# Two fused transformer blocks on one Trainium2 core: up projections as a run of 512-column and a run of 256-column matmuls per weight chunk

## What is computed

```python
# first block
h = rms_norm(x, pre_ffn_norm)
u = causal_dwconv(h @ w_up, conv_w, conv_b)        # w_up: 2048 x 11264
gate, up = jnp.split(u, 2, axis=-1)
y = (jax.nn.gelu(gate, approximate=True) * up) @ w_down
x = x + rms_norm(y, post_ffn_norm)
# second block
up = dwconv3(h @ w_in, w_conv)                     # w_in: 2048 x 11264
gate, val = jnp.split(up, 2, axis=-1)
y = (jax.nn.silu(gate) * val) @ w_out
```

## Time and profile before

| | |
|---|---|
| Median of three runs | 2491.46 us (2490.28 to 2492.52) |
| The profiled execution's own time | 2501.78 us |
| Its span | 2500.0 us, mean granted TensorE clock 0.998 |
| TensorE matmul busy | 2482.6 us, 14809 instructions |
| TensorE weight loads busy | 2108.4 us |
| VectorE, ScalarE, GpSimd busy | 1860.7, 1359.7, 164.2 us |
| Read from HBM | 462.59 MB, 188 GB/s over the span |

### The profile page before, as it was taken

How to read it: one execution, slowest core, us unless ns; L and a number is a source line. 1 busy time by engine, 2 the same in 40 slices (tenths; PEclk the granted TensorE clock), 3 DMA queues, 4 the chain that set the end, 5 groups by cost and what they waited for, 6 DMA issues and landing times.

```text
span 2500.0 us, 37782 instructions
## 1 busy us (share of the span) xinstructions
PE 2482.6 (99%) x14809; PEld 2108.4 (84%) x14809; DVE 1860.7 (74%) x2240; ACT 1359.7 (54%) x1810; POOL 164.2 (7%) x82
## 2 busy tenths in 40 slices
PE   9999999999999999999999999999999999999998
PEld 8888888888888888888888888888888888888886
DVE  6676775787777879888485868775667777678987
ACT  6565664645555555555545455554555555555554
POOL 1000000020111200000000000000012121120000
PEclk9999999999999999999999999999999999999999
DMA  8875445666666666656655555555666666666664
GB/s 239 257 207 151 119 141 185 213 184 186 180 190 186 183 203 223 213 191 207 191 172 168 170 160 170 161 160 180 204 190 190 188 188 189 193 188 224 218 214 158
DMA packets 259266, 470.69 MB, mean 188 GB/s; under 512 B 14520, under 2 KB 56817, under 8 KB 257985
## 3 DMA queue, kind: packets, MB, share of 16 engines
q1 hardware_dynamic: 256897, 457.64, 59.2%
q0 software_dynamic: 2144, 11.30, 1.5%
q10 hardware_dynamic: 96, 0.02, 0.0%
HBM read 462.59 MB, written 6.32 MB: 188 GB/s over the span
## 4 chain that ended last, share of the span: by engine, by line
PE 96%; DVE 1%; DMA 1%; ACT 1%; issue 0%; DVEq 0%; ACTq 0%
PE acc L336 13%; PE tp L336 13%; PE acc L316 7%; PE acc L318 7%; PE acc L317 7%; PE tp L338 7%; PE acc L338 7%; PE acc L1389 4%; PE acc L619 3%; PE acc L618 3%; PE acc L620 3%; PE acc L1391 2%; PE tp L632 1%; PE tp L633 1%; PE tp L634 1%; PE acc L1639 1%
## 5 line engine op out<-in xcount | busy, mean ns | idle before, releaser
L303 DVE TENSOR_TENSOR whl<-raw,whl 128x1024 fp32r<-128x1024 f32 x679 | 877.3, 1301 | 460.1 <-ACT whl L298 458.6
L298 ACT ACTIVATE whl<-raw 128x1024 fp32r<-128x1024 f32 x679 | 717.5, 1060 | 783.9 <-PE acc L338 227.0
L336 PE MATMUL acc<-ahl,whl 128*128 128x512 f32 x1408 | 494.4, 395 | 0.6 <-DVE ahl L421 0.6
L336 PE MATMUL tp<-ahl,whl 128*128 128x512 f32 x1408 | 494.2, 395 | 0.0
L338 PE MATMUL tp<-ahl,whl 128*128 128x256 f32 x1408 | 394.8, 280 | 0.0
L338 PE MATMUL acc<-ahl,whl 128*128 128x256 f32 x1408 | 394.7, 280 | 0.0
L336 PEld LDWEIGHTS acc<-ahl,whl 128*128 128x128 f32 x1408 | 264.0, 187 | 62.8 <-issue 1.0
L336 PEld LDWEIGHTS tp<-ahl,whl 128*128 128x128 f32 x1408 | 263.9, 187 | 61.9
L316 PE MATMUL acc<-whl,ahl 128*128 128x512 f32 x752 | 298.9, 398 | 1.9 <-DVE ahl L2274 1.5
L318 PE MATMUL acc<-whl,ahl 128*128 128x512 f32 x752 | 293.4, 390 | 0.0
L317 PE MATMUL acc<-whl,ahl 128*128 128x512 f32 x752 | 292.8, 389 | 0.0
(11 more groups left out here) (342 smaller groups left out, 3569.8 us busy)
## 6 DMA issues: line engine op xcount, KB each, us to landing
raw<-in_w_up_dram SPq DMA_DIRECT2D x176, 512.0 KB, 4.3
raw<-in_ffn_w_in_dram SPq DMA_DIRECT2D x176, 512.0 KB, 4.3
raw<-in_hgrn_w_in_dram SPq DMA_DIRECT2D x160, 512.0 KB, 3.7
raw<-in_w_in_dram SPq DMA_DIRECT2D x87, 512.0 KB, 3.7
raw<-in_w_down_dram SPq DMA_DIRECT2D x48, 512.0 KB, 5.6
raw<-in_ffn_w_out_dram SPq DMA_DIRECT2D x48, 512.0 KB, 5.7
more<-in_w_down_dram SPq DMA_DIRECT2D x40, 512.0 KB, 5.1
more<-in_ffn_w_out_dram SPq DMA_DIRECT2D x40, 512.0 KB, 5.0
```

What stands on the lines that cost most here:

```text
L298: act.activation(whi[:, s, :], raw[:, s, :], ACT.Copy).then_inc(hi_done, 1)
L303: dve.tensor_tensor(wlo[:, s, :], raw[:, s, :], whi[:, s, :].bitcast(F32), ALU.subtract).then_inc(lo_done, 1)
L336: pe.matmul(o[:, ct % 2, :].rearrange("p (a t) -> p a t", a=2), whi[:, s, c], ahl[:, :, kt, :], start=(kt == 0), stop=False, skip_group_ch ...
```

## The change

`products_turned` is split into two loops. The first goes over both slices and the four `ct` with the eight 512-column matmuls alone; the second goes over the same again with the eight 256-column matmuls. Number, shapes and operands of all matmuls and weight loads stay, and so do the waits of the chunk, which all stand in the first loop. For both up projections this is 352 chunks with 2816 pairs. Lines behind L340 move down by three; the second matmul is now L341.

```diff
                     pe.matmul(o[:, ct % 2, :].rearrange("p (a t) -> p a t", a=2), whi[:, s, c], ahl[:, :, kt, :],
                               start=(kt == 0), stop=False, skip_group_check=True)
-                    mm = pe.matmul(o[:, ct % 2, 0:S], wlo[:, s, c], ahi[:, kt, :], start=False, stop=(kt == KT - 1),
-                                   skip_group_check=True)
+            for k in range(CK):
+                for ct in range(4):
+                    c, o = slice(k * GC + ct * P, k * GC + (ct + 1) * P), part_banks(half, ct // 2)
+                    mm = pe.matmul(o[:, ct % 2, 0:S], wlo[:, s, c], ahi[:, k0 + k, :], start=False,
+                                   stop=(k0 + k == KT - 1), skip_group_check=True)
             mm.then_inc(chunk_used, 1)
```

## The result

| | before | changed |
|---|---|---|
| Median | 2491.41 us (10 executions, 2488.26 to 2498.17) | 2497.65 us (10 executions, 2496.07 to 2500.97) |
| Ratio | 1 | 1.0023, 95% interval 1.0013 to 1.0033 |
| The profiled execution | 2501.78 us, span 2500.0 | 2497.51 us, span 2495.7 |

The changed kernel is slower by 0.23%, about 6 us, where no change was forecast. And yet its profiled execution is 4.3 us shorter than that of before. Both are right, as the experiments show: the time of the kernel before isn't one number.

The account below looks back on a forecast made before the run. TensorE, never idle, was taken to bound the kernel by matmul count times start distance. Timed runs were thought already at the fast beat, so nothing to gain and width changes at 0: 2491.5 us, range 2479 to 2495.

Parts of the forecast that it names:

- part 2: The two width changes left in each chunk: 0 to 0.007 us a chunk, taken as 0; bound 2.3 us over 352 chunks.
- Part 1: Runs of one width in both up projections: steps of 227 and 120 ns, 2.773 us a chunk against 2.827 at the slow beat.
- Part 3: Profiled execution: up1 gains 9 us, up2 nothing; span from 2500.0 to about 2491 us.
- Part 4: Moved waits in the chunk: the remainders' wait 0.48 us earlier at no cost, the row wait at most 0.1 us a projection.
- Part 5: What chunks hand on: signals unchanged, ScalarE and VectorE get chunks 2% sooner than in up1 and keep up.
- From the profiled execution to the timed runs: Timed runs have the fast beat in both projections, the profiled one drew a slow one; median stays 2491.5 us, chance 0.48.
- runs have a dear beat of their own: Rival: weight loads lengthen steps in the runs of both up projections, 18.8 us more, 2510 us; chance 0.12.
- The two rivals with slow beats in the timed runs: Timed runs slow in one up projection, about 2482.5 us, chance 0.32; or in both, 2473 us, chance 0.08.

Follow-up runs that it names:

- wide8: Against the changed kernel, the second matmul of each pair also takes 512 columns, order and runs kept; one execution, 2793.51 us.
- r4: Against the kernel before, four 512-column matmuls then four 256-column ones, twice a chunk; median 2500.87 us, ratio 1.0022.
- r2: Against the kernel before, two 512-column matmuls then two 256-column ones, four times a chunk; median 2495.19 us, ratio 1.0016.
- flip: Against the kernel before, the last pair of each chunk does its 256-column matmul first; median 2503.90 us, ratio 1.0054.

## Why the prediction was wrong, point by point

**The step that failed** is part 2, "the two changes of width left in a chunk", bounded at 0 to 7 ns and taken as 0 "because the fast beat shows alternation that costs nothing". It measured 20.0 ns a chunk, 352 x 0.020 = 7.0 us. The mistake was to share a pair's 6.7 ns out over its two changes. A change of width doesn't have a price that adds up. In strict alternation it may cost nothing; between runs of eight, five dear steps follow it. The upper bound came from the nearest pattern and not from the thing itself.

"No row isolates them" was true of the rows that had been read, not of the trace. The projections hold no such place, but `in1` has a run of eight 256-column matmuls between runs of 512 (with 60 or 30 weight columns and not 128, so not quite the same matmul):

```profile
95.38 1.09 PE L1470 MATMUL tp<-whl,blkhl 128*60 128x256 f32 x8
96.31 0.40 PE L1426 MATMUL acc<-whl,ahl 128*128 128x512 f32 x1
...
98.40 0.39 PE L1426 MATMUL acc<-whl,ahl 128*128 128x512 f32 x1
```

The eight narrow steps take 0.93 us, 0.03 less than at 120 ns, and the nine wide ones behind them 2.09 us, 0.05 more than at 226.7. That is 20 ns net, the price that was missing. Three more places of this kind in `in1` come out by their starts at 18, -6 and 41 ns, so the row would have raised the upper bound well over 7 ns a chunk, and would not have given the number.

**Part 1**, the runs: right in their settled steps (227 and 120 ns), and the sum of 2.773 us is what was missed by those 20 ns.

**Part 3**, the profiled execution: about 2491 us of span forecast, 2495.7 measured. Up1 gave back 33 ns a chunk and not 53, and up2 lost 20. By first and last start that is 5.7 us less and 3.5 us more, 2.2 us net; the other 2.1 us of the 4.3 lie outside the two projections, where nothing was changed.

**Part 4**, the moved waits: right. The wait for the remainders still shows 0.6 us in all. The row wait did come to bind: the first chunk of the up half takes 3.063 us where it took 2.968 at the fast beat, so 0.075 us beside the 20 ns, within the 0.1 allowed. Start by start it is the step behind the fourth matmul, 323 ns long. The weight loads of the changed kernel show who was waited for (busy, mean ns, idle before and its main releaser):

```profile
L336 PEld LDWEIGHTS tp<-ahl,whl 128*128 128x128 f32 x1408 | 253.2, 189 | 45.7 <-DVE uprow L1036 0.5
```

The copy of the row, L1036 here and L1033 in the earlier trace rows, is the only releaser named.

**Part 5**: right. ScalarE and VectorE keep up in all variants: TensorE is busy 400 of 400 us in each stretch shown.

**From the profiled execution to the timed runs**: the 10.3 us between them were indeed one slow beat, 9.2 us, and the batch had hardly any (9 of its 10 executions near 2490 us). This choice was right for the comparison that was made, and by luck: in the last batch 13 of 34 were near 2490. Its reason was not right either. Three near-equal times were read as "they all have the same beats"; three draws had merely come out alike. Over all batches, and by their times, 62 of 116 executions of before had none, 44 had one and 10 had two slow projections, with means of 2490.5, 2498.9 and 2508.3 us. Their mean is 2495.2 us, that of 22 executions of the changed kernel 2497.3. The change is worse by 7 us than a good draw, better by 1.6 us than a middling one, and about 2 us or 0.1% worse on the average. That average hangs on the batches: the changed kernel was slower in the first (ratio 1.0023) and not told apart from before in the last (0.9990, 0.9971 to 1.0009).

**The rivals.** The slower one, "runs have a dear beat of their own", had the right sign and the wrong mechanism: it was to decide by steps above 120 ns in the 256-column run, through weight loads, at 18.8 us. The 256-column steps stay at 120 or below. The dear steps are in the 512-column run, behind the change. It named as its second condition a step above 227 ns there, and that is what the trace has. But its suspect, activations from two places, is cleared by wide8, where the same reads go at 226.7. The two rivals with slow beats in the timed runs describe single executions, not the median of that batch.

The variants that only reorder the same matmuls have medians between 2490.2 and 2503.9 us. The Trainium skill (TensorE: Matmul & The Clock Gate, "Back-to-back issue gap") gives columns over 2.4 GHz plus 2.5 ns for an isolated matmul at the full clock, and for a stream says that a matmul and its weight load together set the distance, with 131 ns sustained at 512 columns. Neither figure looks at the neighbour's width, so by either of them these variants would all take the same time. The traces differ in size too: settled steps of 512 columns are 226.7 ns. The measurement decides.

## What to carry to other kernels

Where TensorE is never idle, take the distance of starts over a few periods of the pattern, and compare stretches that run the same code: two paces in one trace are a sign that the kernel's time may change from one execution to the next, and then three near-equal times prove little. When a term has no row in the stage that is changed, look for one in the others. Price a new order of matmuls by running it, since here the cost of neighbours of different width was a property of the whole repeating pattern. The cheapest order was alternation with the narrow matmul first: 2490.2 us on the average of 22 executions, none above 2492.6, against 2495.2 for the kernel before and 2497.3 for the changed one.

## What was not expected of the hardware

Strict alternation of 512- and 256-column matmuls has two steady paces, 346.7 and 353.3 ns a pair, at the same granted clock of 1.00, and keeps either for some 475 us until something else stands between. Going to 256 columns and back to 512 costs 20 ns net when the runs are of eight or sixteen, 17 when they are of four, 3 when they are of two. Over the fast beat the chunks of the changed kernel, r4, r2, flip and the slow beat are 20.0, 33.3, 13.3, 46.7 and 53.3 ns longer, whole multiples of 6.67 ns. Why it does so is open; the traces show starts, not the reason for them. Open is also what chooses the beat, why the share of executions with a slow one differs between batches (2 of 21 in one, 21 of 34 in another), and why the reversed pair never shows the slow beat behind its last disturbance. In three of its four profiled projections the third chunk took 2.91 us and the fifth 2.86, though both come right behind a block of transposes. That is the price of the slow beat, 0.05 us, so this order isn't immune to it.
